# Another order of attention steps among the steps of a delta rule, in the mixer of a two-layer block

## The reference

```python
def gated_delta_rule(q, k, v, g, beta):          # 4 heads of 128, chunks of 64 tokens
    ...
    sol = lax.linalg.triangular_solve(t_mat, rhs, left_side=True, lower=True, unit_diagonal=True)
    u, w = sol[..., :dv], sol[..., dv:]
    ...
    def step(state, xs):
        q_c, k_c, u_c, w_c, a_c, gl = xs
        v_new = u_c - jnp.einsum('bhcd,bhde->bhce', w_c, state)
        o = jnp.einsum('bhcd,bhde->bhce', q_c, state) + jnp.einsum('bhcm,bhme->bhce', a_c, v_new)
        state = state * jnp.exp(gl)[..., None, None] + jnp.einsum('bhcd,bhce->bhde', k_c, v_new)
        return state, o
```

## Time and profile before

| | |
|---|---|
| median of 3 runs | 2162.65 us (2159.95 to 2166.81) |
| the profiled execution's own time | 2163.42 us |
| its span in the trace | 2161.6 us |
| mean granted TensorE clock | 0.993 |
| PE busy | 2078.6 us (96%) |
| DVE, ACT, POOL busy | 1297.6, 865.7, 223.0 us |
| DMA | 297.47 MB, mean 138 GB/s |

### The profile page before, as it was taken

The page is one execution under the profiler, slowest core; times in us unless marked ns, Lnnn a source line. Parts: engine busy times, 40 slices in busy tenths (PEclk is TensorE's granted clock), DMA queues, the critical chain, the costliest instruction groups (busy, mean ns, idle before and its releaser), DMA issues.

```text
span 2161.6 us, 31542 instructions
## 1 busy us (share of the span) xinstructions
PE 2078.6 (96%) x12313; PEld 1698.6 (79%) x12313; DVE 1297.6 (60%) x2063; ACT 865.7 (40%) x1435; POOL 223.0 (10%) x231
## 2 busy tenths in 40 slices
PE   8988999999989999999999999999999999999997
PEld 7756799877667998877777777888888787777996
DVE  5655677576657774644444468643445834767667
ACT  5423366345333664422222235322222433644442
POOL 2020200000201000000000002200000340623000
PEclk9999999999999999999999999999999999999999
DMA  8477566544775664422221222333332274425662
GB/s 242 156 242 263 143 176 182 187 136 157 253 251 163 181 183 165 140 79 97 59 97 58 97 59 78 101 95 97 97 97 97 85 139 110 63 55 156 194 181 91
DMA packets 304630, 297.47 MB, mean 138 GB/s; under 512 B 10455, under 2 KB 223779, under 8 KB 304401
## 3 DMA queue, kind: packets, MB, share of 16 engines
q1 hardware_dynamic: 297360, 276.92, 41.9%
q0 software_dynamic: 7168, 19.13, 4.0%
HBM read 294.97 MB, written 1.05 MB: 137 GB/s over the span
## 4 chain that ended last, share of the span: by engine, by line
PE 74%; DVE 15%; ACT 3%; DMA 3%; POOL 2%; issue 2%; DVEq 0%; SPq 0%; ACTq 0%; POOLq 0%
PE ps L431 21%; PE ps L433 21%; PE ps L432 21%; DVE w_lo L420 4%; PE ps L1919 2%; PE ps L499 2%; DMA nb<-in_nat_rpb 1%; POOL nb L2301 1%; POOL nb L2305 1%; DVE hid L1541 1%; DMA raw<-in_ada_w 1%; PE ps L708 1%; DVE qkv L1209 1%; PE ps L1902 1%; PE ps L706 1%
## 5 line engine op out<-in xcount | busy, mean ns | idle before, releaser
L420 DVE TENSOR_TENSOR w_lo<-raw,w_hi 128x1024 fp32r<-128x1024 f32 x428 | 525.3, 1269 | 355.7 <-ACT w_hi L412 355.5
L412 ACT ACTIVATE w_hi<-raw 128x1024 fp32r<-128x1024 f32 x428 | 428.7, 1051 | 567.2 <-PE ps L431 467.5
L431 PE MATMUL ps<-zt_hi,w_hi 128*128 128x512 f32 (+1 forms) x816 | 275.3, 337 | 3.9 <-issue 1.5
L433 PE MATMUL ps<-zt_hi,w_lo 128*128 128x512 f32 (+1 forms) x816 | 274.0, 336 | 0.0
L432 PE MATMUL ps<-zt_lo,w_hi 128*128 128x512 f32 (+1 forms) x816 | 273.9, 336 | 0.0
L431 PE MATMUL ps<-xt_hi,w_hi 128*128 128x256 f32 x896 | 256.1, 286 | 11.9 <-DVE w_lo L420 10.3
L432 PE MATMUL ps<-xt_lo,w_hi 128*128 128x256 f32 x896 | 251.8, 281 | 0.0
L433 PE MATMUL ps<-xt_hi,w_lo 128*128 128x256 f32 x896 | 251.8, 281 | 0.0
L431 PEld LDWEIGHTS ps<-xt_hi,w_hi 128*128 128x128 f32 x896 | 169.5, 189 | 20.6 <-DVE w_lo L420 11.2
L431 PEld LDWEIGHTS ps<-zt_hi,w_hi 128*128 128x128 f32 x816 | 153.2, 188 | 24.9 <-issue 2.9
L432 PEld LDWEIGHTS ps<-xt_lo,w_hi 128*128 128x128 f32 x896 | 169.7, 189 | 0.0
(11 more groups left out here) (379 smaller groups left out, 3532.8 us busy)
## 6 DMA issues: line engine op xcount, KB each, us to landing
raw<-in_mlp_w SPq DMA_DIRECT2D x128, 512.0 KB, 4.5
raw<-in_ada_w SPq DMA_DIRECT2D x96, 512.0 KB, 5.7
raw<-in_w_up SPq DMA_DIRECT2D x88, 512.0 KB, 5.2
raw<-in_w_in SPq DMA_DIRECT2D x56, 512.0 KB, 4.9
raw<-in_ret_w_in SPq DMA_DIRECT2D x48, 512.0 KB, 4.5
raw<-in_w_down SPq DMA_DIRECT2D x44, 512.0 KB, 4.2
raw<-in_nat_w_in SPq DMA_DIRECT2D x24, 512.0 KB, 5.2
raw<-in_w_out SPq DMA_DIRECT2D x16, 512.0 KB, 5.9
```

What stands on the lines that cost most here:

```text
L412: nc.scalar.activation(w_hi[:, t, w], raw[:, s, w], ACT.Copy).then_inc(on("w_hi"), act.gives("w_hi"))
L420: ins = nc.vector.tensor_tensor(w_lo[:, t, w], raw[:, s, w], w_hi[:, t, w].bitcast(F32), ALU.subtract)
L431: first = nc.tensor.matmul(out_ap, l_hi, r_hi, start=start, stop=False)
L433: return first, nc.tensor.matmul(out_ap, l_lo, r_hi, start=False, stop=stop)
```

## The change

```diff
--- before.py
+++ after.py
@@ -478,9 +478,9 @@
 
 
         ADA_UNITS = 24
-        ADA_AT = {("mt", 1): 1, "turn": 1, ("mt", 3): 3, ("y", 1): 1, ("x", 1): 2, ("ma", 0): 1, ("mb", 0): 1,
-                  ("x", 2): 1, ("ma", 1): 1, ("x", 3): 1, ("mb", 1): 1, ("x", 4): 1, ("mb", 2): 1, ("x", 5): 1,
-                  "uw": 1, ("mb", 3): 1, ("ov", 0): 1, ("mc", 3): 1, ("ws", 1): 1, ("ov", 1): 1, ("ov", 2): 1}
+        ADA_AT = {("mt", 1): 1, "turn": 1, ("mt", 3): 3, ("x", 1): 2, ("mb", 0): 1, ("mc", 0): 1, ("ma", 1): 1,
+                  ("x", 3): 2, ("mb", 1): 1, ("mc", 1): 1, ("ma", 2): 1, ("x", 5): 2, ("mb", 2): 1, ("mc", 2): 1,
+                  ("ma", 3): 1, ("mb", 3): 1, ("mc", 3): 1, ("ws", 2): 1, ("ov", 2): 1}
         ADA_FIRST = 16
 
         def ada_slot(u):
@@ -514,23 +514,20 @@
         def mixer_steps():
 
             head = ["gram", ("mt", 0), "vt", ("mt", 1), "turn", ("mt", 2), ("mt", 3)]
-            rule = []
-            for n in range(1, 6):
-                rule += [("y", n), ("x", n)]
-            rule += ["uw"]
+            attention = {("y", 1): ("ma", 0), ("y", 2): ("mb", 0), ("x", 2): ("mc", 0),
+                         ("y", 3): ("ma", 1), ("y", 4): ("mb", 1), ("x", 4): ("mc", 1),
+                         ("y", 5): ("ma", 2), "uw": ("mb", 2), ("ws", 0): ("mc", 2),
+                         ("ov", 0): ("ma", 3), ("ws", 1): ("mb", 3), ("ov", 1): ("mc", 3)}
+            rule = [(part, n) for n in range(1, 6) for part in "yx"] + ["uw"]
             for n in range(N_CHUNKS):
                 early = [[], [], ["oa"], ["oc"]][n]
                 rule += [("ws", n)] + [(part, 0) for part in early] + [("ov", n)]
                 if n == 2:
                     rule += [("ob", 0)]
             rule += [("out", 0), ("oa", 1), ("ob", 1), ("oc", 1), ("out", 1)]
-            att = []
-            for g in range(HM // 2):
-                att += [("ma", g), ("mb", g), ("mc", g)]
-            order, rule = head + rule[:1], rule[1:]
-            while rule or att:
-                order += rule[:1] + att[:1]
-                rule, att = rule[1:], att[1:]
+            order = head
+            for step in rule:
+                order += [step] + ([attention[step]] if step in attention else [])
             return order
 
         def hs(h):
@@ -719,10 +716,11 @@
                     for h in range(HG):
                         ins = T.matmul(ps[t][:, hs(h)], k_bg[:, t, hs(h)], xt_inv[:, t, hs(h)], start=True, stop=True)
                     ins.then_inc(on("rule_ps"), pe.gives("rule_ps"))
-                pe.eng.wait_ge(on("uw"), pe.takes("uw", 2))
             elif name == "ws":
                 t, lo = n // 2, CHUNK * (n % 2)
                 half, tok = slice(lo, lo + CHUNK), slice(n * CHUNK, (n + 1) * CHUNK)
+                if n == 0:
+                    pe.eng.wait_ge(on("uw"), pe.takes("uw", 2))
                 pe.eng.wait_ge(on("state" if n else "state0"), pe.takes("state" if n else "state0"))
                 for h in range(HG):
                     ins = T.matmul(ps[4][half, hs(h)], w_t[:, h, tok], state[:, hs(h)], start=True, stop=True)
@@ -1236,7 +1234,7 @@
             dve.used["tok_out"] += 2
             for step in mixer_steps():
                 dve_step(dve, step)
-                if step == "uw":
+                if step == ("mb", 2):
                     split_lo(dve)
                     split_lo(dve)
                 elif step == ("oc", 1):
```

## The result

The changed kernel takes 2141.65 us (median of 4 runs, 2141.47 to 2142.66) against 2163.25 us (median of 4, 2159.95 to 2166.81) before: a ratio of 0.9896, 95% interval 0.9884 to 0.9908, 21.6 us less. The forecast was 2146, 16.5 us less. The profiled execution has a span of 2139.7 us against 2161.6 us.

What follows compares the result with a forecast made beforehand. Bound by latency of attention steps asked for too soon: 19.3 us won in two stretches, less 2 x 0.5 for `mb 0` and about 2.3 for low clock, leaves 16; 2163.4 - 16 = 2147.4, less 0.8 to the median, say 2146 (range 2137 to 2158).

Steps and rivals of the forecast that it cites:

- What bounds it: `y 1` to `out 0`: latency, attention steps asked for too soon after one another; PE idles 12.0 us per layer.
- The new wait: Ahead of the 17th unit, before `uw`: its transfer, issued only after the 15th's use, makes PE wait 2.2 us.
- rival 2: 17th unit lands as slowly as under load, wait 5.7 us, low clock behind it in both layers: 2156 us; chance 0.17.
- Low clock behind it: After the new 2.2 us wait: low clock may follow in one layer; about 2.3 us allowed in the sum.
- `mb 0`: DVE's scalings move under `y 2`, removing the 2.44 us wait; the last may meet GpSimd, 0.5 us per layer counted.
- PE's own work: `y 1` to `out 0`: no instruction added or dropped, so PE's work stays at 76.9 us per layer.
- `ov 3`: Near the stretch's end: some 0.1 us of wait stays ahead of `ov 3`.
- `mb 3`: A unit now also stands ahead, so 1.2 of 2.16 us wait stay, plus 0.2 between its halves.
- `uw`: Wait moved behind 2.1 us of other work, needing 1.17: costs nothing, or 1.17 us per layer without that cover.
- Behind `out 0`: After the stretch PE is busy for all 21 us and its units are asked for 7 to 9 us earlier.
- the likeliest case: Whole kernel: the forecast itself, 2146 us, own range 2141 to 2151, chance 0.52.

Runs made afterwards that it cites:

- e7_unit17: The changed kernel with one of the two conditioning units behind `x 5` moved behind `uw`, so the 17th unit is used later; 2141.36 us, ratio 0.9893.
- e11_x4: e9_ov3 with the unit behind `mb 2` moved behind `x 4`, so the 15th and 16th units are used earlier; 2136.22 us, ratio 0.9866.
- e12_again: The changed kernel itself, unaltered, measured again on another set's chip; 2143.64 us, ratio 0.9899 to the kernel before.
- e6_split: The changed kernel with DVE's two splits put back behind the step `uw`; 2144.44 us, ratio 0.9899 to the kernel before.
- e5_uwback: The changed kernel with TensorE's wait for `uw` put back at the end of `uw`; 2146.75 us, ratio 0.9911 to the kernel before.
- e4_pool: The kernel before with GpSimd's level-4 masks held back until DVE finished the scalings of `mb 0`; 2156.44 us, ratio 0.9955.
- e3_uw: The kernel before with only TensorE's wait for `uw` moved to the head of `ws 0`; 2169.72 us, ratio 1.0022.
- e1_order: The changed kernel with the conditioning units where they stood before and TensorE's wait for `uw` back at its end; 2152.04 us, ratio 0.9933.
- e8_ws1: e7_unit17 with the unit behind `mb 3` moved ahead of it, behind `ws 1`; 2136.50 us, ratio 0.9866 to the kernel before.
- e9_ov3: e8_ws1 with the unit behind `ws 2` moved behind `ov 3`, ahead of `out 0`; 2135.89 us, ratio 0.9862 to the kernel before.

## Why the prediction was right

- *What bounds it*: right. The waits went and the time with them. Idle time per layer was forecast at 4.6 us and was 4.84 and 4.50.
- *The new wait*: right in place, cause and size, 2.48 and 2.16 us against 2.2. e7_unit17 takes it away by using the unit later; e11_x4 shows 7.4 us from issue to use when the unit is asked for 2.1 us behind another, which leans towards the condition of rival 2.
- *Low clock behind it*: it fell in one of two layers, as the sum had it, and lost 1.6 us there (76.81 against 75.20 busy) where 2.3 were allowed. That it was one layer is luck. In e12_again and e6_split it fell in both, in e5_uwback in one: 6 of 8 such waits, of 2.16 to 2.49 us, were followed by it.
- *`mb 0`*: the mechanism stood in the prediction and e4_pool shows it. The 0.5 us for a second meeting was not needed: DVE's last scaling began 0.32 us ahead of GpSimd's operation and ended as it started. That margin is small, so the half wait was a fair term that happened not to fall due. At `ma 0` the scalings met GpSimd's `k_dec` operations (line 950), not level 3 as forecast. Still DVE left `ma 0` at 7.0 and its subtractions ended at 9.4, against 7.0 and 9.5 in the forecast. By the rule of the Trainium skill (SBUF — State Buffer, Who interferes with whom), whoever of GpSimd and a DVE in a two-port mode issues first holds the shared ports for its whole instruction. The rows of `ma 0` agree with it: GpSimd started first (126.30 against 126.53), and DVE's scaling ended 0.03 us behind GpSimd's operation and took 0.67 us longer than without it. At `mb 0` it is hardly put to the test.
- *PE's own work*: the term that was mis-sized, and the step behind it was wrong. I had 76.9 us per layer for the old order, which e4_pool confirms (76.79 at full clock), and carried it over: no instruction is added or dropped, so the work stays. It did not stay; in the new order it is 75.20 us. Distances between starts, less the waits, show where 1.6 us went. The four `mb` took 4.2 us in the old order and take 3.4 in the new one: `mb 0` 0.80 us (132.80 to 133.60), `mb 1` and `mb 2` 0.75, and `mb 3`, which still waits, 1.13. Two pairs of units that now stand back to back take 1.85 us each where two single ones take 2.0, 0.3 us in all. Most of the rest lies in the steps that stood just ahead of a wait, each about 0.1 us shorter when the next step follows at once.
- *`ov 3`*: 0.1 us forecast, none found. *`mb 3`*: 1.4 us forecast in two parts, 1.42 found.
- *`uw`*: the wait is right at 1.18 us (e5_uwback). Its price in time is open: e5_uwback lost some 3 us, not clear of noise, and e3_uw won nothing.
- *Behind `out 0`*: I had the gain kept there and it was. That 0.6 us more is won in each layer, since the low clock behind `out 0` is gone, was not in the sum.

Together: the two stretches were forecast at 163.0 us, or 166.3 with the allowances for `mb 0` and the clock, and took 161.4, 5.0 us less; 1.2 us were won behind `out 0` and 0.8 ahead of and between the mixers, 1.1 us lost at the end. That is 5.9 us, which is how far the profiled execution (2141.5) lay under its own forecast (2147.4). Of it 3.4 us are PE's work, taken as fixed (76.9 against 75.2 us in each layer). The median came out 4.4 us under the forecast, inside the stated range and just at the low end of the likeliest case's own (2141 to 2151).

What the 21.0 us won in the two stretches consist of: 14.7 us less idle time, 3.2 us less work at full clock, and 3.1 us less low clock (3.1 and 1.6 us before, none and 1.6 after). The last part differs from execution to execution.

What the change is made of: the order, with the splits' place, is worth 13 us alone; the units' places are worth some 5 us in the new order (e1_order against e5_uwback, whose intervals just overlap) and cost 16 us in the old one; the moved wait some 3 us in the new order, not clear of noise. They are no sum of independent parts.

## What to carry to other kernels

In a step list that all engines walk in order, price a step's place by what TensorE has to do between the step that starts a chain and the one that needs its end; a wait of 1 us is filled by 1 us of work moved ahead of it, until the slowest engine's own chain is the bound (e8_ws1, then e9_ov3). Work that feeds on a ring of buffers can't be moved freely: count for each unit which use releases its slot, on which engine, and how much lies between that and its own use (2.2 us of wait for being one step too near, 8.9 us for a loop through a second engine). A duration read from an instruction that had waited is not its duration in a full queue (1.13 against 0.75 us for the transposes of an `mb`), so taking waits away also shortens the work around them.

## What was not expected of the hardware

The length of a single wait does not tell whether the low clock follows: 2.48 us in layer one was not followed by it, 2.16 us in layer two was, with the same steps around them, and before the change it followed 0.54 and 0.83 us ahead of `out 0` in layer two, where the rows behind are slow:

```profile
649.59 1.08 PE L743 MATMUL ps<-a_mat,att 64*64 64x128 f32 x8 [0.54 <-DVE a_mat L1392]
651.51 0.97 PE L749 MATMUL ps<-cst,attn 128*128 128x128 f32 x4 [0.83 <-DVE attn L1437]
```

And the same kernel met it once in one profile and twice in the next (2139.7 and 2142.3 us of span). In these profiles it goes with the spread between runs, and in the profiled execution of e3_uw it is why less idle time came with a longer stretch.
